# Third branch of a decoder layer: gate product with tokens on partitions, x turned to rows ahead of it

## The reference, cut to what matters

```python
x = x + mix @ w_out[i]
h = rms_norm(x, norm_ffn[i])
u = causal_dwconv(h @ w_up[i], conv_w[i], conv_b[i])
...                                        # x += (gated u) @ w_down[i]
x += sigmoid(rms_norm(x, norm_ple[i]) @ w_pg[i]) * (p[i] @ w_pe[i])
return rms_norm(x, norm_final)             # rms_norm(x, g) = x * rsqrt(mean(x*x) + eps) * g
```

## Time and profile before

| what | value |
|---|---|
| time, median of 3 runs (lowest, highest) | 750.39 us (748.95, 751.5) |
| the profiled execution: its time, its span | 747.16 us, 745.4 us |
| PE busy | 723.8 us, 97% |
| DVE, ACT, POOL busy | 453.2, 314.2, 122.4 us |
| mean granted TensorE clock | 0.993 |

### The profile page before, as it was taken

The page is one execution under the profiler, slowest core; times in us unless marked ns, Lnnn a source line. Parts: engine busy times, 40 slices in busy tenths (PEclk is TensorE's granted clock), DMA queues, the critical chain, the costliest instruction groups (busy, mean ns, idle before and its releaser), DMA issues.

```text
span 745.4 us, 10529 instructions
## 1 busy us (share of the span) xinstructions
PE 723.8 (97%) x3935; PEld 592.6 (80%) x3935; DVE 453.2 (61%) x705; ACT 314.2 (42%) x545; POOL 122.4 (16%) x99
## 2 busy tenths in 40 slices
PE   5999999998999999999999999999999999999993
PEld 4778777877888878778888888888888888888883
DVE  4754779748866645576767676676763333324555
ACT  7652214255665634444333343433332223226344
POOL 1030000025655432201011101101110001000000
PEclk9999999999999999999999999999999999999998
DMA  8333221312222102333332323333215332333202
GB/s 263 113 89 112 58 58 57 118 53 85 86 86 86 58 29 85 113 107 92 97 102 85 112 84 107 90 94 103 85 49 163 98 105 79 99 113 113 86 0 114
DMA packets 121745, 69.44 MB, mean 93 GB/s; under 512 B 2658, under 2 KB 118450, under 8 KB 121706
## 3 DMA queue, kind: packets, MB, share of 16 engines
q1 hardware_dynamic: 119982, 65.72, 29.4%
q10 hardware_dynamic: 1724, 3.19, 1.3%
HBM read 66.77 MB, written 2.13 MB: 92 GB/s over the span
## 4 chain that ended last, share of the span: by engine, by line
PE 88%; DVE 5%; ACT 3%; issue 1%; DMA 1%; SPq 0%; POOL 0%; DVEq 0%; ACTq 0%
PE bank L466 26%; PE bank L468 26%; PE bank L467 26%; PE bank L506 2%; PE bank L606 2%; DVE w_lo L1161 2%; PE bank L588 2%; PE bank L574 1%; DMA raw<-in_w_in 1%; ACT w_hi L834 1%; PE bank L576 1%; DVE h_lo L1167 1%; DVE x_t L1252 1%; PE bank L540 1%; ACT scratch L852 1%
## 5 line engine op out<-in xcount | busy, mean ns | idle before, releaser
L466 PE MATMUL bank<-h_hi,w_hi 128*128 128x512 f32 (+1 forms) x664 | 264.3, 398 | 2.6 <-DVE h_lo L1167 2.6
L468 PE MATMUL bank<-h_hi,w_lo 128*128 128x512 f32 (+1 forms) x664 | 257.8, 388 | 0.0
L467 PE MATMUL bank<-h_lo,w_hi 128*128 128x512 f32 (+1 forms) x664 | 257.7, 388 | 0.0
L834 ACT ACTIVATE w_hi<-raw 128x1024 fp32r<-128x1024 f32 (+1 forms) x116 | 120.8, 1042 | 288.2 <-PE bank L468 288.1
L1161 DVE TENSOR_TENSOR w_lo<-raw,w_hi 128x1024 fp32r<-128x1024 f32 (+1 forms) x116 | 144.7, 1247 | 113.0 <-ACT w_hi L834 112.8
L466 PEld LDWEIGHTS bank<-h_hi,w_hi 128*128 128x128 f32 x664 | 125.1, 188 | 28.6 <-DVE w_lo L1161 2.8
L468 PEld LDWEIGHTS bank<-h_hi,w_lo 128*128 128x128 f32 x664 | 125.1, 188 | 26.2
L467 PEld LDWEIGHTS bank<-h_lo,w_hi 128*128 128x128 f32 x664 | 125.3, 189 | 24.2 <-issue 1.0
L1647 POOL TENSOR_SCALAR probs<-probs,row_inv 128x512 f32<-128x512 f32 (+3 forms) x48 | 66.0, 1379 | 148.4 <-DVE row_inv L1432 148.1
L466 PE MATMUL bank<-act_hi,w_hi 128*128 128x512 f32 x176 | 68.6, 389 | 0.0
L468 PE MATMUL bank<-act_hi,w_lo 128*128 128x512 f32 x176 | 68.5, 389 | 0.0
(11 more groups left out here) (186 smaller groups left out, 791.7 us busy)
## 6 DMA issues: line engine op xcount, KB each, us to landing
raw<-in_w_up SPq DMA_DIRECT2D x44, 512.0 KB, 3.6
raw<-in_w_in SPq DMA_DIRECT2D x30, 512.0 KB, 3.7
raw<-in_w_down SPq DMA_DIRECT2D x16, 512.0 KB, 3.2
raw<-in_w_out SPq DMA_DIRECT2D x8, 512.0 KB, 3.3
raw<-in_w_pg SPq DMA_DIRECT2D x8, 512.0 KB, 3.3
bias<-bias_table ACTq DMA_DIRECT2D x6, 512.0 KB, 3.7
raw<-in_w_down SPq DMA_DIRECT2D x8, 384.0 KB, 2.8
x_rows<-in_x SPq DMA_DIRECT2D x4, 512.0 KB, 5.8
```

The source lines that it names most:

```text
L466: pe.matmul(bank, hi, x_hi, start=first, stop=False)
L467: pe.matmul(bank, hi, x_lo, start=False, stop=False)
L468: return pe.matmul(bank, lo, x_hi, start=False, stop=last)
L834: act.activation(w_hi[:, u % SPLIT, 0:nk * ncol], raw[:, u % RAW, 0:nk * ncol], ACT.Copy)\
```

## The change

- **w_pe and w_pg** are used the other way round: a unit of w_pg is now two k steps of 512 columns, p and h are stationary (128 tokens at a time) and the weights are moving. Products come out with tokens on partitions, in eight pieces g = (c, t): feature half c (512 features), token tile t. Each piece of w_pg needs four units, and each unit serves four pieces, so five of the eight units get tiles of their own (`pg_hi`, `pg_lo`) in space that act_hi and act_lo leave, and three reuse w_hi and w_lo.
- **x is turned to rows** before the gate product: after every second piece of w_pe PE transposes two feature tiles (`turn_rows`, 8 transposes); DVE copies the even ones and ACT the odd ones into `y_rows`.
- **The third norm's squares**: ACT squares the four row tiles with a sum per token (`root_of_tokens`); the squares of x_t on ACT, the sums on POOL and `sum_squares(2)` go. The root is one number per token, hence per partition, and becomes the scale of ACT's sigmoid, which reads the product in PSUM; DVE's multiplication by `r_row` goes.
- **The end**: x is updated in rows, ACT squares each updated piece, and there is no transpose behind the gate. Roots of tiles 0 and 1, and of tile 2, are taken by 13 small operations on DVE without Ln and Exp (`root_of`), that of tile 3 by Ln and Exp. Only the last piece is cut in halves, by columns. ACT scales columns 0 to 511 of a tile and DVE columns 512 to 1023. Tile 3 is stored in two halves.
- `gain_row` lies in conv_v and is loaded during w_down's stage, behind a wait on `act_ready`.

The tiles keep their sizes in steps of 256 bytes: the 16 numbers of `tok` come out of the filler `after_small`.

The diff, cut to its core:

```diff
-for _f in range(KT):
-    _unit("w_pg", 0, KT, _f * P)
-    _group("ple", _f)
+for _c in range(2):
+    for _k0 in range(0, KT, 2):
+        _unit("w_pg", _k0, 2, _c * 512, 512)
...
+OWN_PG = 5
+PIECES = 2 * SEQ // P
...
-        gain_row = sb("gain_row", [P, D])
+        pg_hi = sb("pg_hi", [P, OWN_PG, 1024], F32R)
+        pg_lo = sb("pg_lo", [P, OWN_PG, 1024], F32R)
+        gain_row = conv_v[:, 0:2, :].rearrange("p a n -> p (a n)")
...
+            if w < OWN_PG:
+                return pg_hi[:, w, :], pg_lo[:, w, :]
+            return w_hi[:, (PG + w) % SPLIT, :], w_lo[:, (PG + w) % SPLIT, :]
...
+            return banks[6 if g == PIECES - 1 and cols.start else g % TT][:, cols]
...
-                if u == PG + RAW:
-                    sp.wait_ge(unit_done, PE_UNITS)
-                    sp.dma_start(gain_row[:, :], a["norm_final"].rearrange("(o d) -> o d", o=1).to_broadcast([P, D]))\
+                    sp.wait_ge(act_ready, FT)
+                    sp.dma_start(gain_row, a["norm_final"].rearrange("(o d) -> o d", o=1).to_broadcast([P, D]))\
                       .then_inc(gain_in, 16)
-            for t, done, count in ((0, y_dve, 1), (1, y_act, 1), (2, y_dve, 2), (3, y_act, 2)):
-                sp.wait_ge(done, count)
+            for t in range(TT - 1):
+                sp.wait_ge(y_act, t + 1)
+                sp.wait_ge(y_dve, t + 1)
                 sp.dma_start(out[0, t * P:(t + 1) * P, :], y_rows[:, t, :]).then_inc(stored, 16)
...
+            t = TT - 1
+            for done, cols in ((y_act, slice(0, 512)), (y_dve, slice(512, D))):
+                sp.wait_ge(done, TT)
+                sp.dma_start(out[0, t * P:(t + 1) * P, cols], y_rows[:, t, cols]).then_inc(stored, 16)
+            sp.wait_ge(stored, 16 * (TT + 1))
...
-                if u == PE_UNITS:
-                    sum_squares(2)
...
-            def turn_result(f):
-                pe.wait_ge(x_ready, 2 * KT + f + 1)
...
-                for t in range(TT):
-                    mm = pe.transpose(banks[(2, 3, 6)[f % 3]][:, t * P:(t + 1) * P], x_t[:, f, t * P:(t + 1) * P], ident)
-                mm.then_inc(y_turned, 1)
...
+            def token_products(bank, x_hi, x_lo, m_hi, m_lo, first, last):
+                pe.matmul(bank, x_hi, m_hi, start=first, stop=False)
+                pe.matmul(bank, x_hi, m_lo, start=False, stop=False)
+                return pe.matmul(bank, x_lo, m_hi, start=False, stop=last)
+            def turn_rows(j):
...
+                pe.wait_ge(x_ready, KT + 2 * j + 2)
+                if j:
+                    pe.wait_ge(rows_dve, j)
+                    pe.wait_ge(rows_act, j)
+                for f in (2 * j, 2 * j + 1):
+                    for t in range(TT):
+                        mm = pe.transpose(turned[f % 2][:, t * P:(t + 1) * P], x_t[:, f, t * P:(t + 1) * P], ident)
+                    mm.then_inc(rows_turned, 1)
...
+            for n in range(PIECES):
+                c, t = n // TT, n % TT
+                u = PE_UNITS + c
+                if t == 0:
+                    pe.wait_ge(wlo_ready, u + 1)
+                if c:
+                    pe.wait_ge(pe_kept, n - 3)
+                tokens = slice(t * P, (t + 1) * P)
+                for k in range(2):
+                    cols = slice(k * 512, (k + 1) * 512)
+                    mm = token_products(banks[PE_BANK[t]][:, :], p_hi[:, k, tokens], p_lo[:, k, tokens],
+                                        w_hi[:, u % SPLIT, cols], w_lo[:, u % SPLIT, cols], k == 0, k == 1)
+                mm.then_inc(unit_done if t == TT - 1 else pe_done, 1)
+                if n % 2:
...
+            for g in range(PIECES):
...
+                for cols in (slice(0, 512),) if g < PIECES - 1 else (slice(0, 256), slice(256, 512)):
+                    for k in range(KT):
+                        w = 4 * c + k // 2
+                        if t == 0 and k % 2 == 0:
+                            pe.wait_ge(wlo_ready, PG + w + 1)
...
+                        mm = token_products(pg_bank(g, cols), h_hi[:, k, tokens], h_lo[:, k, tokens], hi[:, at], lo[:, at],
+                                            k == 0, k == KT - 1)
+                    mm.then_inc(pg_done, 1)
...
-                    square_x(n)
+                    if n < KT:
+                        square_x(n)
...
+                sums, guess = stat[:, 0, :], stat[:, 2, :]
+                act.wait_ge(rows_act, KT // 2)
+                act.wait_ge(rows_dve, KT // 2)
+                for t in range(TT):
...
+                    act.activation(scratch[:, 2:4, :].rearrange("p a n -> p (a n)"), y_rows[:, t, :], ACT.Square,
+                                   accum_out=sums[:, t:t + 1]).then_inc(tok_var, 1)
+                act.wait_ge(tok_var, TT)
+                act.activation(guess, sums, ACT.Ln, bias=eps_col[:, :], scale=1.0 / D).then_inc(tok_ln, 1)
...
+                act.activation(guess, guess, ACT.Exp, scale=-0.5).then_inc(tok_guess, 1)
...
+            for n in range(PIECES):
+                keep_pe(n)
+                if n % 2:
+                    keep_rows(n)
+                else:
+                    split_pg(n // 2)
+            root_of_tokens()
...
+            act.preload_act_table(ACT.Sigmoid)
+            split_pg(4)
+            act.wait_ge(tok_newton, 4)
+            for g in range(PIECES - 1):
+                sigmoid_of(g, g, whole)
+                if g < TT - 1:
+                    split_pg(5 + g)
+                if g == PIECES - 2:
+                    scale_rows(0, y_root, 1)
+                    scale_rows(1, y_root, 1)
+                square_of(g, g, whole)
+            sigmoid_of(PIECES - 1, PIECES - 1, left)
+            square_of(PIECES - 1, PIECES - 1, left)
+            sigmoid_of(PIECES - 1, PIECES, right)
             act.preload_act_table_set("natural_log_exp_and_others")
...
+            square_of(PIECES - 1, PIECES, right)
+            scale_rows(2, y_root, 2)
...
+            act.activation(stat[:, 2, t:t + 1], stat[:, 3, t:t + 1], ACT.Ln, bias=eps_col[:, :], scale=1.0 / D).then_inc(y_ln, 1)
...
+            act.activation(stat[:, 2, t:t + 1], stat[:, 2, t:t + 1], ACT.Exp, scale=-0.5).then_inc(y_guess, 1)
+            scale_rows(t, y_root, 3)
...
+                dve.wait_ge(tok_var, TT)
+                dve.tensor_scalar(v, stat[:, 0, :], 1.0 / D, EPS, ALU.mult, ALU.add).then_inc(tok_newton, 1)
...
+                dve.scalar_tensor_tensor(out=r_tok[:, :], in0=t, scalar=-3.0, in1=guess, op0=ALU.add, op1=ALU.mult)\
...
+                dve.tensor_tensor(conv_g[:, g % 3, cols], conv_g[:, g % 3, cols], pe_out[:, t, here], ALU.mult).then_inc(gated, 1)
+                dve.wait_ge(gated, n + 1)
+                dve.tensor_tensor(y_rows[:, t, here], y_rows[:, t, here], conv_g[:, g % 3, cols], ALU.add).then_inc(y_added, 1)
...
+            def root_of(t0, t1):
...
+                dve.wait_ge(y_squared, TT + t1)
+                link(dve.tensor_tensor(v, last_parts[:, t0:t1, 0], last_parts[:, t0:t1, 1], ALU.add))
+                link(dve.tensor_scalar(v, v, 1.0 / D, EPS, ALU.mult, ALU.add))
...
+                for step in range(3):
+                    y0 = first if step == 0 else guess
+                    link(dve.tensor_tensor(t, v, y0, ALU.mult))
...
+            for n in range(0, PIECES, 2):
+                keep_rows(n)
+                split_pg(n // 2)
+            root_of_tokens()
+            split_pg(4)
+            for g in range(PIECES - 1):
+                add_gated(g, g, whole)
+                if g < TT - 1:
+                    split_pg(5 + g)
+                if g == 1:
+                    dve.wait_ge(gain_in, 16)
+                if 1 <= g <= TT:
+                    gain_rows(g - 1)
+                if g == 5:
+                    root_of(0, 2)
+                    finish_rows(0, y_root, 1)
+            finish_rows(1, y_root, 1)
+            root_of(2, 3)
+            add_gated(PIECES - 1, PIECES - 1, left)
+            add_gated(PIECES - 1, PIECES, right)
+            finish_rows(2, y_root, 2)
+            t = TT - 1
+            y, v, guess, turn = (stat[:, n, t:t + 1] for n in range(4))
+            dve.wait_ge(y_squared, PIECES + 1)
+            dve.tensor_reduce(out=stat[:, 3, t:t + 1], in_=last_parts[:, t:t + 1, :], axis=mybir.AxisListType.X, op=ALU.add)\
+               .then_inc(mean_sum, 1)
+            dve.wait_ge(mean_sum, 1)
+            dve.tensor_scalar(v, stat[:, 3, t:t + 1], 1.0 / D, EPS, ALU.mult, ALU.add).then_inc(mean_ready, 1)
+            dve.wait_ge(mean_ready, 1)
+            dve.wait_ge(y_guess, 1)
+            dve.tensor_tensor(turn, v, guess, ALU.mult).then_inc(tok_newton, 1)
+            dve.wait_ge(tok_newton, 5)
+            dve.scalar_tensor_tensor(out=turn, in0=turn, scalar=-0.5, in1=guess, op0=ALU.mult, op1=ALU.mult).then_inc(tok_newton, 1)
+            dve.wait_ge(tok_newton, 6)
+            dve.scalar_tensor_tensor(out=y, in0=turn, scalar=1.5, in1=guess, op0=ALU.add, op1=ALU.mult).then_inc(y_root, 1)
```

(3 more changed lines are left out.)

308 lines of the change are left out of this document (119 added, 189 removed).

## The result

The changed kernel takes 743.5 us (median of 4 runs, 742.8 to 744.5), the kernel before 749.7 us on the same chip (4 runs, 748.95 to 751.5): ratio 0.992, interval 0.9903 to 0.9937, that is -6.2 us. Forecast were -3.2 us and 747.2 us.

What follows compares the result with a forecast made beforehand. PE was taken to bound the kernel up to its last product, then a tail and stores; PE's -1.2 and the tail's -2.0 gave -3.2 us, 750.39 to 747.2 us, range 744.4 to 750.2 (8 in 10).

Steps and rivals of the forecast that it cites:

- `sum_squares(2)`, -0.9: w_pe's stage on PE: the third norm's matmul by ones with its changeovers goes, saving 0.9 us.
- Transposes, 8 x 0.50 = 4.0: PE ahead of w_pg: eight groups of four transposes in four pairs, 0.50 us each, 4.0 us (bounds 2.9 to 4.2).
- PE's stream, -1.2: PE from w_pe's first product to its end: ends at 732.35 against 733.57, -1.2 us (-1.0 to -2.3).
- No wait on PE, slack 0.8 at the second turn: Transposes beside w_pe: ACT's and DVE's copies come in time, cost 0, with 0.8 us cover on ACT.
- Third norm off the path: ACT's four squares, Ln, Exp at w_pg's start: first piece's sigmoid three us late, caught up by piece 2, no cost.
- The tail, 5.9 behind PE's stream: Small operations behind PE's last product: last value at 738.2, 5.9 us behind PE's stream instead of 7.9, saving 2.0 us.
- The stores, unchanged at 3.9 (bounds -0.6 to +0.4): Output stores behind the last value: three of 512 KB and two of 256 KB still take 3.9 us.
- 1 (the tail gives nothing back): Tail: DVE and ACT hand-overs take two us more, only PE's 1.2 us are left: 749.2 us, chance 0.25.
- 2 (ACT sets the pace): Beside w_pe: ACT's turned-tile copies take 3 us, PE waits 4.0 us in all: 751.2 us, chance 0.06.
- 3 (the clock falls beside the turns): w_pe's stage: half of the 48 products run at the lower TensorE clock, 5.8 us: 753.0 us, chance 0.04.
- 4 (more than forecast): Tail and stores: right half's sigmoid not late and half stores land in 2.6 us: 744.6 us, chance 0.07.
- The table load: ACT in the tail, between last sigmoid and last square: 1.28 us, without the skill's drain of 1.38 us more.

Runs made afterwards that it cites:

- e_turn_twice: Changed kernel with every transpose of turn_rows made twice in a row (32 more transposes): 747.12 us (10 runs), +3.50 us to PE's end.
- e_pair: Changed kernel with the last tile stored whole and tile 2's store held back until tile 3 is done: 745.02 us (4 runs), stores 4.3 us.
- e_whole_store: Changed kernel with its last tile stored as one 512 KB transfer instead of two of 256 KB: 743.70 us (6 runs), stores 3.0 us.
- e_gate_first: Changed kernel with the last piece's left gating ahead of the 13-link root of tile 2 on DVE: 742.47 us (6 runs), ratio 0.991.
- c_before: The kernel before, without an edit, measured again: 750.46 us (10 runs), ratio 1.001.

## Why the prediction was wrong, point by point

- **Moving weights cost nothing.** Right: 0.227 us.
- **`sum_squares(2)`, -0.9.** Right, 0.85.
- **Transposes, 8 x 0.50 = 4.0.** Too high: w_pe's stage gives 14.42 - 10.89 = 3.5, and e_turn_twice 8 x 0.44 = 3.5 for transposes alone, so in pairs hardly anything is left for changeovers. Of the two rows, 0.36 and 0.52, I had chosen the one with the changeover of a single group of four in it. That 0.52 is a mean over five and holds one group that started 0.17 us late (0.64); the other four cost 0.47 to 0.51. Term mis-sized by 0.5, inside its bounds.
- **PE's stream, -1.2.** 58.76 forecast, 58.35 measured, -1.6.
- **No wait on PE, slack 0.8 at the second turn.** Right: 0.9.
- **Third norm off the path.** Right, with 7.6 us to spare.
- **gain_row's load.** Right: PE does not wait in w_down's stage.
- **The tail, 5.9 behind PE's stream.** 5.84. Right in order and length, the late right sigmoid (1.1 forecast, 0.9 measured) too.
- **The stores, unchanged at 3.9 (bounds -0.6 to +0.4).** Wrong: -0.9, outside the bounds. I read the 3.9 as what a last store takes and looked for the change in its size. The landings of 2.6 to 3.5 held the answer: of two stores in a row the first landed in 2.6 and the second, issued 0.4 us behind it, in 3.5. The last one was of the second kind (e_pair brings it back), and the tail's new order parts the two. The half stores, which I had reasoned on, do nothing (e_whole_store).
- **The sum.** -3.2 was forecast; -4.5 is the change: -0.4 and -0.9 are the two terms above. This is shown by three profiles of the kernel before and four of the changed one, which agree within 0.1 us each, and by the lower heaps. The bounds of the difference, which I gave as -5.0 to -2.0, come to -4.9 and -2.6 when the terms' own bounds are added up.
- **From the sum to a time.** The last step failed by more than any term, and without it the same range, 2.1 us lower, would have held 743.5. I wrote that the profiled execution is 3.2 us below the median and applied the difference to the median. The three runs shown had two in the upper heap, so 750.39 stood 2.1 us above the heap to which most runs of both kernels belong. 748.3 - 3.2 would have been 745.1. With the two terms it is 743.8.
- **The rivals.** 1 (the tail gives nothing back) did not come: the 26 links ran about 0.2 us apart and the tail came out at 5.84. 2 (ACT sets the pace) did not: its slack was as forecast. 3 (the clock falls beside the turns) did not, even with 64 transposes. Its price was also too high: I took the difference of two passages through the array, 0.63 - 0.39, where the distance from start to start counts, 0.43 (15.21 to 15.64 in the same timeline) against 0.23, so 24 x 0.20 = 4.8 us. By the Trainium skill ("TensorE: Matmul & The Clock Gate", Part 4: PE-mode transpose) transposes do not count as PE being busy the same way as products; in this kernel, with products between the turns, no run shows an effect of it. 4 (more than forecast) was right in sign for another reason. It wanted an early right sigmoid, which came 0.9 us late, and short half stores. These did land in 2.0 and 2.2 us, but one after the other, and the end came no earlier than with one whole store (e_whole_store). Its 744.6 does not follow from its prices either: 1.1 for the sigmoid and 0.9 for a landing of 2.6 in place of 3.5 give 745.2.
- **The table load.** The square starts at 736.66, 0.02 us behind the end of the load at 736.64. The drain of 1.38 us that the Trainium skill ("ScalarE: Activation LUTs", What ACT_TABLE_LOAD costs) gives is not seen here either.

## What to carry to other kernels

Count the difference of two profiles from the first place where their code differs, and see what heap the runs of a base belong to before applying a difference to their median: here the region repeated within 0.1 us while its start scattered by 3.5. Ask of the last wait (a store behind the last value) not only how long it takes but what stands in its queue with it. And halving the last piece only pays if nothing else stands ahead of the first half on the engine that takes it up: with the 13 links ahead of it the halves lost 0.58 us against one piece, and with the links behind it (e_gate_first) they won 0.29.

## What the runs showed of the hardware

- A wait of 2.0 us of TensorE in the middle of a stretch at full clock is in some executions followed by some us of low clock (0.87, 0.50 and 0.78 in three windows of 2 us in c_before), and in others of the same kernel not at all (4 of the 16 profiles in which it stands show it). Filling it with matmuls whose result nobody uses costs nothing: median 743.8 with it, 743.85 without.
- Two stores of 512 KB issued together put the end 4.3 us behind the last value; one alone, 3.0. The first lands in 2.6 us and the one behind it in 3.4 to 3.5.
- 128x128 fp32 transposes in one row run 0.11 us apart (0.44 for four) with a granted clock of 1.00, 64 of them within 18 us (e_turn_twice).
- The low clock behind the first h matmul at 15 us does not last equally long in every execution: 0.96 over the first 40 us in seventeen profiles, 0.91 in three, and 1.2 us more from there to w_pe.
